# Sixteen attention heads in pairs on the halves of the TensorE array, in a shorter pipeline of slots

## The reference

```python
o_c, p_c = cmp_attention(q, k_cmp, v_cmp, qpos)
o_s = sel_attention(q, qpos, idx, ok, slc_all[:, :, 0], slc_all[:, :, 1], n_sel)
o_w = window_attention(q, qpos, win_all[:, :, 0], win_all[:, :, 1], win_pos)
o_n = g[..., 0:1] * o_c + g[..., 1:2] * o_s + g[..., 2:3] * o_w
mix = jnp.concatenate([o_g.reshape(B, T, GLA_WIDTH), o_n.reshape(B, T, NSA_WIDTH)], axis=-1).astype(h.dtype)
```

## Time and profile before

| | |
|---|---|
| median of 3 runs | 2824.31 us (2822.68 to 2824.48) |
| profiled execution | 2824.61 us, its span 2822.4 us |
| the slots' loop | from 1425.4 to 1684.2 us of the span |
| TensorE busy in the span | 2718.7 us (96%), mean granted clock 0.958 |
| VectorE, ScalarE, GpSimd busy | 1563.6, 460.6, 762.9 us |

### The profile page before, as it was taken

The page is one execution under the profiler, slowest core; times in us unless marked ns, Lnnn a source line. Parts: engine busy times, 40 slices in busy tenths (PEclk is TensorE's granted clock), DMA queues, the critical chain, the costliest instruction groups (busy, mean ns, idle before and its releaser), DMA issues. The chain is left out here.

```text
span 2822.4 us, 45319 instructions
## 1 busy us (share of the span) xinstructions
PE 2718.7 (96%) x17691; PEld 2606.0 (92%) x17691; DVE 1563.6 (55%) x1539; ACT 460.6 (16%) x1106; POOL 762.9 (27%) x564
## 2 busy tenths in 40 slices
PE   8999999999999999999799989899999999999997
PEld 7999999899999979999477769789999999999996
DVE  5555556455555665554355565565565565565555
ACT  2110001111000140000344560131100000000002
POOL 1331332133133630000211034443223313323352
PEclk9999999999999999999777999989999999999998
DMA  6555555455555435674322316435455455555552
GB/s 185 149 154 159 149 148 145 129 149 158 157 149 149 133 97 154 180 149 119 119 91 75 104 42 147 111 105 149 134 164 149 136 162 149 140 143 163 149 138 78
DMA packets 735573, 384.97 MB, mean 136 GB/s; under 512 B 65546, under 2 KB 729994, under 8 KB 735194
## 3 DMA queue, kind: packets, MB, share of 16 engines
q1 hardware_dynamic: 735386, 384.17, 49.7%
q10 hardware_dynamic: 128, 0.05, 0.0%
HBM read 372.24 MB, written 16.00 MB: 138 GB/s over the span
## 5 line engine op out<-in xcount | busy, mean ns | idle before, releaser
L316 PE MATMUL bank<-xh_before,wh_before 128*128 128x320 f32 x2112 | 657.6, 311 | 14.0 <-DVE wl_before L334 13.9
L317 PE MATMUL bank<-xl_before,wh_before 128*128 128x320 f32 x2112 | 656.1, 311 | 0.0
L318 PE MATMUL bank<-xh_before,wl_before 128*128 128x320 f32 x2112 | 655.8, 311 | 0.0
L316 PE MATMUL bank<-xh_after,wh_after 128*128 128x320 f32 x1664 | 521.4, 313 | 23.7 <-DVE wl_after L334 15.2
L332 DVE CAST wh_before<-raw 128x2048 fp32r<-128x2048 f32 (+1 forms) x196 | 219.9, 1122 | 579.8 <-PE bank L318 537.6
L317 PE MATMUL bank<-xl_after,wh_after 128*128 128x320 f32 x1664 | 518.4, 312 | 0.0
L318 PE MATMUL bank<-xh_after,wl_after 128*128 128x320 f32 x1664 | 518.3, 311 | 0.0
L334 DVE TENSOR_TENSOR wl_before<-raw,wh_before 128x2048 fp32r<-128x2048 f32 (+1 forms) x196 | 463.5, 2365 | 6.7
L332 DVE CAST wh_after<-raw 128x2048 fp32r<-128x2048 f32 (+1 forms) x168 | 184.9, 1101 | 437.2 <-PE bank L318 435.3
L316 PEld LDWEIGHTS bank<-xh_before,wh_before 128*128 128x128 f32 x2112 | 399.6, 189 | 15.8 <-issue 12.3
L334 DVE TENSOR_TENSOR wl_after<-raw,wh_after 128x2048 fp32r<-128x2048 f32 (+1 forms) x168 | 409.5, 2438 | 5.8
(11 more groups left out here) (239 smaller groups left out, 3253.2 us busy)
## 6 DMA issues: line engine op xcount, KB each, us to landing
raw<-in_w_ffn_in SPq DMA_DIRECT2D x176, 1024.0 KB, 5.6
raw<-in_w_ffn_out SPq DMA_DIRECT2D x128, 704.0 KB, 4.9
raw<-in_w_in SPq DMA_DIRECT2D x36, 1024.0 KB, 5.5
raw<-in_w_in SPq DMA_DIRECT2D x16, 512.0 KB, 5.2
raw<-in_w_out SPq DMA_DIRECT2D x16, 512.0 KB, 4.4
raw<-in_w_out SPq DMA_DIRECT2D x64, 128.0 KB, 4.2
proj<-in_cache_cmp_kv SPq DMA_DIRECT2D x64, 64.0 KB, 2.4
raw<-in_state_gla SPq DMA_DIRECT2D x8, 512.0 KB, 3.5
```

Source lines behind the costliest of these rows:

```text
L316: pe.matmul(out, L.wh[a][:, w], hi[:, k], start=(k == 0), stop=False)
L317: pe.matmul(out, L.wh[a][:, w], lo[:, k], start=False, stop=False)
L318: last = pe.matmul(out, L.wl[a][:, w], hi[:, k], start=False, stop=(k == nk - 1))
```

## The change

The 32 prompt items become 16 **pairs**: two heads that share keys in the two halves of the array's rows. The list `units` has 8 pairs of `qt` 0, and then 8 times a sequence and a pair of `qt` 1: 24 units, 25 slots. Both heads of a pair go through each step together: score products alternate between rows 0 to 63 and 64 to 127 and between two of three banks (0, 1, 5), output products between the halves of the columns; DVE and ACT treat small operands of both heads at once. The second head's three products on the probabilities are POOL's (`scale`), and so are the query products of GLA (`levels`). The state products of GLA alternate between the halves of the rows.

The pipeline is shorter. PE computes the scores of the next unit (`scores(i + 1)`) in slot i, and `turn(i - 1)`, `take(i - 1)`, `outputs(i - 1)` and `out(i - 1)` all belong to the slot after the unit's own; `RING` is 2, and the turned probabilities and the output have one buffer each. A pair of `qt` 1 is turned in two goes over bank 3. A slot holds both a level (`gla_level`) and a sample's state (`gla_rest`), so GLA's levels take 9 slots and not 17. The norm's four small products move from POOL to DVE, as single instructions over the four heads.

```diff
-    k_one = [L.sb(f"k_one{i}", [NS, GH * P], scope=s) for i in range(2)]
+    k_one = [L.sb(f"k_one{i}", [P, GH * P // 2], scope=s) for i in range(2)]
...
+    NV, RING = 2, 2
...
+    PR = L.sb("probs", [P, RING, 2, 2 * GW + 16], scope=s)
+    PT = L.sb("probs_turned", [P, 2, 5, P], scope=s)
...
-    items = [(p, a, g, qt) for qt in range(2) for p in range(2) for g in range(G) for a in range(2)]
...
-    NI = len(items)
-    SLOTS = NI + LAG + 1
+    units = [("pair", p, g, 0) for p in range(2) for g in range(G)]
+    for n in range(8):
+        units += [("seq", n), ("pair", n // G, n % G, 1)]
...
+    SLOTS = NU + 1
...
+    def goes(i):
+
+        return 2 if units[i][0] == "pair" and units[i][3] else 1
...
+    ring, ring_at, last_user, frees = (0, 1, 5), {}, {}, {}
+    for i in range(NU):
+        for a in range(heads(i)):
+            r = ring[len(ring_at) % len(ring)]
+            ring_at[i, a], frees[i, a] = r, last_user.get(r, 0)
+            last_user[r] = exp_no[i] + 3 * a + 2
+
+    def main(i, a):
+
+        w = min(width(i), PAST)
+        return bank[ring_at[i, a]][:, 0:2 * w].rearrange("p (n k) -> p n k", n=2)
...
+                to = [claim(("state", b, j)) for j in range(2)]
+                for h in range(2):
+                    for j in range(2):
+                        r = slice(j * NS, (j + 1) * NS)
+                        mm = pe.matmul(to[j][0][:, h * DV:(h + 1) * DV], k_one[b % 2][r, h * P:(h + 1) * P],
+                                       v_gla[r, 2, (2 * j + h) * DV:(2 * j + h + 1) * DV], start=True, stop=True)
+                        if h:
+                            mm.then_inc(to[j][1], 1)
...
-                        pe.matmul(main[:, n * w:(n + 1) * w], qT, proj[r, T_KV + 4 + 4 * n + p, 0:w],
-                                  start=True, stop=True)
+                        for a in range(2):
+                            r = slice(a * HD, (a + 1) * HD)
+                            pe.matmul(main(i, a)[:, n], proj[r, T_NQ + 4 * p + g, qt * P:(qt + 1) * P],
+                                      proj[r, T_KV + 4 + 4 * n + p, 0:w], start=True, stop=True)
                     if i:
                         pe.wait_ge(masked, 2 * i)
-                    pe.matmul(small[:, 32:48], qT, k_cmp[r, NB, p], start=True, stop=True).then_inc(scored, 1)
+                    pe.matmul(small[:, 0:32], proj[:, T_NQ + 4 * p + g, qt * P:(qt + 1) * P],
+                              k_pair[:, p].rearrange("p a n -> p (a n)"), start=True, stop=True).then_inc(scored, 1)
...
+            def turn(i, go):
+                if turn_no["p", i, go]:
+                    pe.wait_ge(taken, turn_no["p", i, go])
+                w, x = PR[:, i % RING], bank[4]
                 chunks = min(width(i), PAST) // P
-                for n in range(2):
-                    at = WIN + 16 if n and i in seq else n * WIN
-                    for g in range(chunks):
-                        pe.transpose(bank[3][:, (chunks * n + g) * P:(chunks * n + g + 1) * P],
-                                     w[:, at + g * P:at + (g + 1) * P], ident)
-                if i in seq:
-                    pe.transpose(x[0:32, 2 * P:3 * P], w[:, NEW:NEW + 32], ident)
-                pe.transpose(x[0:16, P:2 * P], w[:, CMP:CMP + 16], ident).then_inc(turned, 1)
+                for a in range(heads(i)) if goes(i) == 1 else (go,):
+                    pe.wait_ge(weighed_pool if a else weighed, (pairs[i] if a else i) + 1)
+                    for n in range(2):
+                        at = WIN + 16 if n and seq(i) is not None else n * WIN
+                        for c in range(chunks):
+                            m = chunks * n + c + (2 * chunks * a if goes(i) == 1 else 0)
+                            mm = pe.transpose(bank[3][:, m * P:(m + 1) * P], w[:, a, at + c * P:at + (c + 1) * P], ident)
+                if go == goes(i) - 1:
+                    if i >= 1:
+                        pe.wait_ge(out_taken, i)
+                    for a in range(heads(i)):
+                        mm = pe.transpose(x[0:16, (1 + a) * P:(2 + a) * P], w[:, a, CMP:CMP + 16], ident)
+                    if seq(i) is not None:
+                        mm = pe.transpose(x[0:32, 2 * P:3 * P], w[:, 0, NEW:NEW + 32], ident)
+                mm.then_inc(turned, 1)
...
+                            for a in range(2):
+                                at = (3 + 2 * n) * 256 + (2 * p + a) * HD
+                                pe.matmul(x[a * HD:(a + 1) * HD, 0:P], L.kv_tok[:, c, at:at + HD],
+                                          PT[:, a, chunks * n + c], start=(n == 0 and c == 0), stop=False)
+                    for a in range(2):
+                        kv = 2 * p + a
+                        mm = pe.matmul(x[a * HD:(a + 1) * HD, 0:P], v_small[32:48, NB, kv * HD:(kv + 1) * HD],
+                                       PT[32:48, a, 4], start=False, stop=True)
+                    mm.then_inc(out_ready, 1)
...
+            scores(0)
             for i in range(SLOTS):
-                for n in range(2):
-                    if i + 2 - n in seq:
-                        turn_keys(seq[i + 2 - n], n)
-                if i < NI:
-                    scores(i)
-                if LAG <= i < NI + LAG:
-                    turn(i - LAG)
-                if i > LAG:
-                    outputs(i - LAG - 1)
-                gla_step(i)
+                gla_level(i)
+                if i >= 1:
+                    turn(i - 1, 0)
+                if i + 1 < NU:
+                    scores(i + 1)
+                if i >= 1 and goes(i - 1) == 2:
+                    turn(i - 1, 1)
+                gla_rest(i)
+                if seq(i + 2) is not None:
+                    turn_keys(seq(i + 2), 0)
+                if i >= 1:
+                    outputs(i - 1)
+                if seq(i + 2) is not None:
+                    turn_keys(seq(i + 2), 1)
 
...
-            def q_level(lv):
-                dve.wait_ge(made_e, lv + 1)
-                if lv >= 2:
-                    await_made(dve, last_score(lv - 1))
-                dve.tensor_tensor(halves(QL, lv)[0], halves(q, lv)[0], halves(D_[lv % 2], lv)[0], ALU.mult
-                                  ).then_inc(made_q, 1)
...
+                    dve.tensor_tensor(all_t, all_var, all_r, ALU.mult).then_inc(o_step, 1)
+                    dve.wait_ge(o_step, 1)
+                    dve.tensor_tensor(all_t, all_t, all_r, ALU.mult).then_inc(o_step, 1)
+                    dve.wait_ge(o_step, 2)
+                    dve.tensor_scalar(all_t, all_t, -0.5, 1.5, ALU.mult, ALU.add).then_inc(o_step, 1)
+                    dve.wait_ge(o_step, 3)
+                    dve.tensor_tensor(all_r, all_r, all_t, ALU.mult).then_inc(o_step, 1)
...
+                    cm = L.cst[:, K_CAUSAL:K_CAUSAL + P]
+                    for a in range(2):
+                        x = main(i, a)[:, :, w - P:w]
+                        ins = dve.tensor_tensor(x, x, cm.unsqueeze(1).to_broadcast([P, 2, P]), ALU.add)
+                    ins.then_inc(masked, 1)
...
+            def scale(i):
+                st, wd, w = stat[i % RING], width(i), PR[:, i % RING, 0]
+                dve.wait_ge(summed, 3 * i + 3)
+                dve.tensor_scalar(w[:, 0:wd], w[:, 0:wd], st[:, 3, 0, 1:2], None, ALU.mult)
+                dve.tensor_scalar(w[:, WIN:WIN + wd], w[:, WIN:WIN + wd], st[:, 3, 0, 2:3], None, ALU.mult)
+                dve.tensor_scalar(w[:, CMP:CMP + 16], w[:, CMP:CMP + 16], st[:, 3, 0, 0:1], None, ALU.mult
+                                  ).then_inc(weighed, 1)
...
+                if i < NU:
+                    maxima(i)
+                if i >= 1:
+                    weights(i - 1)
+                    scale(i - 1)
...
+            def scale(i):
+                st, wd, w = stat[i % RING], width(i), PR[:, i % RING, 1]
+                pool.wait_ge(summed, 3 * i + 3)
+                pool.tensor_scalar(w[:, 0:wd], w[:, 0:wd], st[:, 3, 1, 1:2], None, ALU.mult)
+                pool.tensor_scalar(w[:, WIN:WIN + wd], w[:, WIN:WIN + wd], st[:, 3, 1, 2:3], None, ALU.mult)
+                pool.tensor_scalar(w[:, CMP:CMP + 16], w[:, CMP:CMP + 16], st[:, 3, 1, 0:1], None, ALU.mult
+                                   ).then_inc(weighed_pool, 1)
...
+            def levels(lv):
+                k_level(lv)
+                pool.tensor_tensor(halves(QL, lv)[0], halves(q, lv)[0], halves(D_[lv % 2], lv)[0], ALU.mult
+                                   ).then_inc(made_q, 1)
...
-                if i < O_STEP and i % 2 == 0 and i // 2 < LAST:
-                    k_level(i // 2 + 1)
+                if i >= 1 and heads(i - 1) == 2:
+                    scale(i - 1)
+                if i < LAST:
+                    if i == 0:
+                        pool.wait_ge(chain_d, 4 + GH)
...
+                if i < 2 * GH:
+                    if i == 0:
+                        pool.wait_ge(acted, 3)
```

(92 more changed lines are left out.)

405 lines of the change are left out of this document (190 added, 215 removed).

## The result

| | before | after |
|---|---|---|
| median | 2823.45 us (10 runs) | 2829.99 us (10 runs, 2823.91 to 2835.5) |
| ratio | | 1.0027, 95% interval 1.0016 to 1.0039 |
| profiled execution, span | 2824.61, 2822.4 us | 2827.73, 2825.9 us |
| loop of slots | 258.8 us | 264.0 us |
| TensorE busy, mean clock | 2718.7 us, 0.958 | 2684.1 us, 0.954 |

The change makes the kernel 0.27% slower, some 7 us, where 6.8 us of gain were forecast. A second series of the same changed kernel, run later beside other kernels, gave 2830.85 us and 1.0026 (1.0014 to 1.0038).

The account below looks back on a forecast made before the run. PE was taken to bound both stages before, one slot's chain through DVE, ACT and PE after. Stage 1 -16.3, stage 2 +7 and small things +2.5 gave -6.8: 2818 us from 2824.6; own case 2806 to 2831, with rivals 2790 to past 2850.

Parts of the forecast that it names:

- What bounds the kernel: Loop of slots: PE bounds both stages before; after the change, one slot's chain through DVE, ACT and PE decides.
- State products in two halves: GLA's state products: row halves run beside each other, so eight take 1.0 us a slot, with 1.99 as other bound.
- Stage 1: Loop up to the end of GLA's levels: 117.2 us, 16.3 less than 133.5, at a clock between its levels.
- POOL's block: Stage 1: POOL's products hold up DVE's steps, at least once a slot, +1.0 us; bounds 0 and 2.6.
- small things: `k_pair`'s zeroes and copies, doubled `v_gla` rows and split `k_new` +0.5 us, hops between engines +2.
- stage 2's sum: Loop after GLA's levels: eight periods 111 us, other steps +24, last period -5, passage +2; 132 against 125.3, 7 more.
- the plain period of 13.9 us: Stage 2, two slots: pair's slot 7.25 us plus sequence's slot 6.65, with ACT and PE taking turns.
- +24: Stage 2: GLA's outputs, final state, means, reciprocals and norm products, 32 us now stopping the ping-pong, a quarter hidden.
- Rival (b): Stage 2: gaps lower PE's clock, six of eight periods at 1.2 GHz, +29, 2847 us; chance 0.20.
- Rival (a): Stage 1: PE at full clock, 2801 us, or POOL's products fall into waits, down to 2790; chance 0.20.
- (c): Both stages: products on the halves do not run together at all, +25 us and a small rest, 2844; chance 0.08.
- (d): Pair outputs: column halves do not run together, only row halves; 1.0 us more in eight slots, 2826; chance 0.10.

Follow-up runs that it names:

- the filled kernel: Changed kernel plus unread products on PE where it waits, from slot 13 on (256 columns ahead of turnings, 512 ahead of a sequence's outputs): 2820.73 us, ratio 0.9989.

## Why the prediction was wrong

*What bounds the kernel* was read rightly: the length of a slot's chain took PE's place. *State products in two halves*: right, 1.13 us for my 1.0. *Stage 1*: 119.7 us for my 117.2, with the clock at 0.75, near the middle that I took. But PE is busy 81% of it where I had 60 to 70, and POOL's block costs little (below), so that the sum came out near is in part luck. The *small things*, +2.5, do not show: the loop starts at 1423.6 us and not at 1425.4, which is within what executions differ by.

*The step that failed is stage 2's sum*, "stage 2: 132 against 125.3". It was made at 2.4 GHz throughout, and its base was right only there: the plain period of 13.9 us is measured as 13.7 with the clock held at 1.00, and as 16.3 in the change. Over the last part the clock costs 7 us in the profiled execution (99.3 less 91.9) and 15 in the second (107.0 less 91.9); both are estimates and rather low, since the filled kernel is at 0.96 and carries its filling. That alone turns -6.8 into no gain or a loss. The rest of the miss is the second term, "+24": in the filled kernel the five periods with other steps are 12.6, 8.9, 1.3, 4.1 and 1.8 us over 13.7, together 28.7, of which a little is still clock. With both, 132 becomes 132 + 7.4 + 4.7 = 144.1 us, and 144.3 were measured. My sign that the period is too short, waits of PE that end on DVE's scaling in stage 2 too, was there (some 14 us), but the period was not too short at full clock.

Rival (b) named this mechanism and its place. Its price, +29, was too high, since it had six of eight periods wholly at 1.2 GHz, where the last part has a mean of 0.77 or 0.66. What I held against it was the wrong reading: that the stage "has such gaps now and keeps 0.95". Before, PE is idle 6 of 125 us in it; in the change 25 of 144. Gaps are not all that goes with a low clock, however: stage 1 before had PE busy 130.4 of 133.5 us at 0.72, and what lowers it there no run shows.

Rival (a) is out: stage 1's clock rose only from 0.72 to 0.75, and though most of POOL's block fell into waits, stage 1 did not get shorter than the forecast. (c) and (d) are out by the rows above: sixteen output instructions on alternate column halves take the 1.09 us of eight. The Trainium skill's rule in "TensorE: Matmul & The Clock Gate", Part 3 (The mechanism), on which (d) rested, that weight loads overlap only where rows differ, does not show here: these products use the same rows, and the measurement decides. Nor was it right that the trace of before forbids nothing of it. Its page has PE and the weight loads (PEld) busy at the same time for most of the span, and most of them have operands of 128 rows and 128 columns:

```profile
PE 2718.7 (96%) x17691; PEld 2606.0 (92%) x17691; DVE 1563.6 (55%) x1539; ACT 460.6 (16%) x1106; POOL 762.9 (27%) x564
```

POOL's block was described wrongly, though stage 1 came out near. In the timelines of POOL and of DVE in one slot of stage 1:

```profile
1490.82 0.70 POOL L1585 TENSOR_SCALAR probs<-probs,stat 128x128 f32<-128x128 f32 x1 [6.59 <-DVE stat L1515]
...
1492.37 1.26 POOL L1579 TENSOR_TENSOR xT<-proj 128x512 f32<-128x512 f32 x1
1493.59 1.71 POOL L1592 TENSOR_TENSOR xT<-proj 128x512 f32<-128x512 f32 x1
...
1492.65 1.53 DVE L1396 TENSOR_TENSOR proj<-xT 128x512 f32<-128x512 f32 x1
1494.10 1.74 DVE L1397 TENSOR_TENSOR proj<-xT 128x512 f32<-128x512 f32 x1
...
1498.48 1.66 DVE L1423 SCALAR_TENSOR_TENSOR raw<-raw,decay_samples,bank 128x256 f32<-128x256 f32 x4 [2.64 <-PE bank L1184]
```

A scaling of 128 columns takes POOL 0.60 or 0.70 us, above my upper bound of 0.44. DVE's differences take 1.5 to 1.7 us beside POOL's products (0.69 in the kernel before, L1350), and each ends some 0.55 us after the product beside it. That is a block of 1.9 us a slot, nearer to my upper bound of 2.6 than to 1.0. But behind it DVE waits 2.64 us for the state, so the block has cover here, and the 2.6 a slot by which stage 1 would have gained only 3.5 us did not come: it gained 13.8.

## What to carry to other kernels

Work taken from a bound engine is only worth what the next wait leaves of it, and on TensorE gaps can cost by themselves: price the pieces on the chain at the lower clock too, and not only at the one that the stage has while it is busy. Packing products and shortening the pipeline are two changes. Here one slot of distance put back made the changed kernel 0.6% faster, and with DVE's query products put back too, the same packing beats both kernels, by 0.5 and 0.8%. Of the packing alone, in the old pipeline, only the state products were tried; they gave some 0.1%, with an interval that nearly reaches no change. Pairs of heads in the old pipeline were not tried. When one kernel's runs spread, compare the clock of the same stretch first: the same code took 99.3 and 107.0 us.

## What was not expected

- The changed kernel's runs go with their mean clock: in the first series 2824 to 2828 us at 0.954 or 0.955 and 2832 to 2836 at 0.949 or 0.950, with nothing else changed.
- Products on the two column halves run beside each other with the same rows: sixteen instructions in the time of eight, 1.09 us.
- A part of the kernel whose code is the same can lose what another part gains: with packed states the last part went from 86.6 to 91.5 us, at a clock of 0.87 for 0.92.
- POOL's first scaling of a pair takes 0.70 us for 128 columns and 1.08 for 256: not in proportion to L1553's 1.09 for 320, though these ran beside DVE.
